# A gated delta recurrence on Trainium2: the level products of the inverses on 32x32 diagonal blocks instead of 64x64

## The chip, the core and the metric

The kernel runs on one core of a Trainium2 chip. The core has a matrix engine (TensorE, PE in the profile), which loads a stationary operand (PEld) and streams another through it into PSUM; VectorE (DVE), ScalarE (ACT) and GpSimd (POOL) for elementwise work; and SyncE (SP), which here only starts DMAs. The metric is the device time of the whole program in microseconds. All numbers are fp32.

## The reference

The program computes two blocks of two layers each on 1024 latent and 256 context tokens of width 1024. The first block's layers mix three branches; one is a bidirectional recurrence over the tokens, with 6 heads of 64 x 64 state, run forward and backward. Only this branch is touched:

```python
def _rwkv7_step(S, inp):
    r, w, k, v, kk, b = inp
    sa = jnp.einsum('bhvk,bhk->bhv', S, kk)
    S = S * w[:, :, None, :] - sa[..., None] * b[:, :, None, :] + v[..., None] * k[:, :, None, :]
    return S, jnp.einsum('bhvk,bhk->bhv', S, r)

def _rwkv_bidir(rin, S0_f, S0_b):
    r, decay, kd, v, kk, bd = rin
    S_f, y_f = lax.scan(_rwkv7_step, S0_f, (r, decay[:, :, 0], kd[:, :, 0], v, kk, bd[:, :, 0]))
    S_b, y_b = lax.scan(_rwkv7_step, S0_b, (r, decay[:, :, 1], kd[:, :, 1], v, kk, bd[:, :, 1]),
                        reverse=True)
    return S_f, S_b, y_f + y_b
```

## The kernel before

`rwkv_core` runs the recurrence once in each of the two layers of the first block. It cuts the 1280 tokens into chunks of 64 (`CH`), and takes them in 10 blocks of two chunks, with the forward and the backward direction (`d`) side by side. The heads go in three pairs (`g`, `NP = 3`); `h` is the head in its pair, `q = 2 d + h`, and `c` the chunk, which lies on 64 of the 128 partitions (`half[c]`).

Within a chunk the steps depend on each other through a strictly triangular 64x64 matrix A, and (1 + A) must be inverted. The kernel builds the inverse by doubling: level 0 is the identity with the 2x2 blocks' entries; level `lv` joins diagonal blocks of size 2^lv into ones of twice the size. `TU` holds for each q the current inverse T and its transpose U, `ML` the entries of A which belong to each level, cut out with masks by GpSimd (L2033). A level is

- `level_w` (L1778): W = (masked A)T, then ScalarE copies it from PSUM to `Ws` (L1942),
- `level_d` (L1793 and L1796): the two products of W with U, for T and for U, after which VectorE subtracts them from `TU` (L1971).

There are six levels (`NLEV = 6`), level 0 in GpSimd and 1 to 5 on TensorE; at level 5 only U is brought up to date. Around them a block has: `grams` (L1729), the products of the scaled keys that give A and three further 64x64 matrices, for the next block; `turned` (L1742, L1745), eight 128x128 transposes per head pair; `start_t` (L1753), T as the transpose of U at level 0; `bv` (L1764); `solve` (L1806), the inverse times X; `outputs` (L1826 to L1841), the products that make the block's transfer matrices; and `state` (L1857, L1865), which applies the block before to the carried state and its outputs.

Each engine's program is written out by hand, in the order in which the functions `block_of` call the steps; nothing reorders it. On TensorE the ten blocks are unrolled completely. A level is W of pair 0, W of pair 1, D of 0, W of 2, D of 1, D of 2; the state's first half follows level 1 and its second level 3, and the three gram groups of the next block follow levels 2 to 4. Semaphores are counted waits: `pw`/`aw` between W and ScalarE, `pd`/`dl` between D and VectorE, `pn`/`dh` and `py`/`dy` for the state. SyncE loads a block's operands (`rk_in`, six DMAs of 384 KB, and smaller ones) as soon as the outputs two blocks earlier are done.

## Time and profile before

| | |
|---|---|
| median of 3 runs | 4876.69 us (4873.02 to 4878.9) |
| profiled execution, its span | 4866.1 us |
| TensorE matmuls busy | 4241.5 us, 87% |
| TensorE weight loads busy | 3280.6 us, 67% |
| VectorE busy | 2749.5 us, 57% |
| ScalarE, GpSimd busy | 1537.1 us, 1475.8 us |
| instructions recorded | 103654 |

The profile is of one execution; its own time isn't recorded apart from the span, and the median of the runs lies 10.6 us above the span. The two recurrences run in the stretches from about 555 to 1030 us and from 2118 to 2592 us. "PE" counts matmuls from first column in to last out, so that several overlap in the array and a busy TensorE is not one at its peak: how closely starts follow each other tells more. A line such as `L1793 ... 64*64 64x64 x4` is a group of four records with a 64x64 stationary operand and 64 rows by 64 columns streamed. "issue" as a releaser means that the engine waited for nothing that the profile shows. Instructions reach the engines from memory through DMA queues of their own, queue 8 among them.

### The profile page before, as it was taken

The numbers are of one execution on the slowest core, as the hardware profiler recorded it, in microseconds if no ns is written. First come the engines' busy times: TensorE is split into PE (matmuls) and PEld (weight loads), VectorE is DVE, ScalarE is ACT, GpSimd is POOL, SyncE is SP. The second block draws the span as 40 slices with busy tenths as digits, with TensorE's granted clock in tenths as the row PEclk, the third lists the DMA queues.
The fourth block names the chain that finished last, engine by engine and source line by source line (L and its number), as shares of the span: only waits on it lengthen the run. The fifth ranks groups of instructions, "written<-read, shape, count | busy, mean of one in ns | idle before, by whom it ended". The sixth has DMA issues, their size and how long they took to land. (4 is left out here: it accounts for less than half of the span.)

```text
span 4866.1 us, 103654 instructions
## 1 busy us (share of the span) xinstructions
PE 4241.5 (87%) x43026; PEld 3280.6 (67%) x43026; DVE 2749.5 (57%) x4666; ACT 1537.1 (32%) x2721; POOL 1475.8 (30%) x1090
## 2 busy tenths in 40 slices
PE   6999889877998799989986998689788988978898
PEld 4887688854667587778884666578545677854566
DVE  3465444455666447544445665665575656557565
ACT  1332222223552123222222553210155421015542
POOL 2232233302013323233331111565232135523213
PEclk8999999988999899989998999789899999989999
DMA  6455532342135445642324133533403253340325
GB/s 194 146 186 189 145 78 59 81 159 83 42 83 178 148 153 198 197 122 71 78 59 148 45 92 112 172 99 106 149 7 81 67 183 124 104 142 17 81 53 181
DMA packets 517941, 561.41 MB, mean 115 GB/s; under 512 B 112732, under 2 KB 412284, under 8 KB 515380
## 3 DMA queue, kind: packets, MB, share of 16 engines
q1 hardware_dynamic: 389876, 475.93, 31.6%
q10 hardware_dynamic: 127616, 78.95, 5.6%
q8 instruction: 348, 5.70, 0.5%
q14 instruction: 101, 0.83, 0.1%
HBM read 366.75 MB, written 192.23 MB: 115 GB/s over the span
## 5 line engine op out<-in xcount | busy, mean ns | idle before, releaser
L1096 PE MATMUL pr_acc<-hH,pr_wh 128*128 128x512 f32 (+1 forms) x1288 | 482.4, 375 | 0.0
L1097 PE MATMUL pr_acc<-hL,pr_wh 128*128 128x512 f32 (+1 forms) x1288 | 466.0, 362 | 0.0
L1098 PE MATMUL pr_acc<-hH,pr_wl 128*128 128x512 f32 (+1 forms) x1288 | 465.6, 361 | 0.0
L2586 ACT ACTIVATE an_p<-an_p,an_stat 128x1280 f32<-128x1280 f32 (+5 forms) x372 | 339.7, 914 | 162.8 <-DVE an_stat L2664 157.2
L2033 POOL TENSOR_TENSOR rk_ml<-rk_lmask,rk_g 128x384 f32<-128x384 f32 x240 | 232.1, 999 | 464.1 <-DVE rk_g L1963 464.1
L2526 PE MATMUL an_t<-ident,an_p 128*128 128x128 f32 x2152 | 319.5, 283 | 40.3 <-ACT an_pT L2593 27.8
L2619 POOL TENSOR_TENSOR an_kl<-an_k,an_kh 128x1280 fp32r<-128x1280 f32 (+3 forms) x36 | 78.5, 2179 | 898.5 <-DVE an_qh L2644 898.5
L2526 PEld LDWEIGHTS an_t<-ident,an_p 128*128 128x128 f32 x2152 | 236.7, 142 | 163.9 <-issue 68.0
L2660 DVE CUSTOM_DVE_ANT_0 an_p<-an_s,an_mask 128x256 f32<-128x256 f32 (+8 forms) x308 | 274.9, 892 | 101.7 <-PE an_s L2509 68.4
L1971 DVE TENSOR_TENSOR rk_tu<-rk_tu,rk_ps 128x512 f32<-128x512 f32 x300 | 190.3, 634 | 237.0 <-PE rk_ps L1796 237.0
L1465 POOL TENSOR_TENSOR sp_sl<-sp_w,sp_sh 128x512 fp32r<-128x512 f32 x172 | 246.0, 1437 | 196.8 <-DVE sp_sh L1540 178.4
L2551 PE MATMUL an_oacc<-an_pT,an_v 128*64 128x512 f32 (+3 forms) x1224 | 298.1, 562 | 4.0 <-DVE an_pT L2671 1.9
L1374 PE MATMUL sp_acc<-sp_ch,sp_sh 128*128 128x512 f32 x728 | 285.5, 392 | 7.6 <-POOL sp_sl L1465 7.6
L1140 POOL TENSOR_TENSOR pr_wl<-pr_w,pr_wh 128x1024 fp32r<-128x1024 f32 x58 | 142.7, 2461 | 470.1 <-DVE pr_wh L1160 470.1
L1375 PE MATMUL sp_acc<-sp_cl,sp_sh 128*128 128x512 f32 x728 | 285.1, 392 | 0.0
L1376 PE MATMUL sp_acc<-sp_ch,sp_sl 128*128 128x512 f32 x728 | 284.9, 391 | 0.0
L1096 PEld LDWEIGHTS pr_acc<-hH,pr_wh 128*128 128x128 f32 x1288 | 245.4, 191 | 58.0 <-issue 20.5
L2593 ACT COPY an_pT<-an_t 128x512 f32<-128x512 f32 (+3 forms) x356 | 186.2, 540 | 297.2 <-PE an_t L2526 296.3
L1796 PE MATMUL rk_ps<-rk_tu,rk_ws 64*64 64x64 f32 x4800 | 276.7, 219 | 3.5 <-issue 3.3
L1097 PEld LDWEIGHTS pr_acc<-hL,pr_wh 128*128 128x128 f32 x1288 | 245.3, 190 | 38.0 <-issue 1.0
L1098 PEld LDWEIGHTS pr_acc<-hH,pr_wl 128*128 128x128 f32 x1288 | 244.6, 190 | 38.1
L2671 DVE COPY an_pT<-an_t 128x512 f32<-128x512 f32 (+3 forms) x256 | 155.7, 616 | 178.5 <-PE an_t L2526 176.0
(382 smaller groups left out, 10181.1 us busy)
## 6 DMA issues: line engine op xcount, KB each, us to landing
CHK<-ri_out SPq DMA_DIRECT2D x24, 1920.0 KB, 8.1
rk_in<-CHK SPq DMA_DIRECT2D x120, 384.0 KB, 5.9
pr_w<-in_w_in ACTq DMA_DIRECT2D x58, 512.0 KB, 4.1
UT<-pr_out SPq DMA_DIRECT2D x45, 640.0 KB, 4.6
sp_w<-in_w_in ACTq DMA_DIRECT2D x50, 512.0 KB, 5.2
U<-sp_c SPq DMA_DIRECT2D x100, 256.0 KB, 2.0
mod_w<-in_w_mod SPq DMA_DIRECT2D x16, 1024.0 KB, 8.0
mo_w<-in_w_out SPq DMA_DIRECT2D x16, 1024.0 KB, 9.6
```

The costliest lines, as they stand in the source:

```text
L1096: nc.tensor.matmul(out, wh[:, u, k, 0:m], hi, start=(k == 0), stop=False)
L1097: nc.tensor.matmul(out, wh[:, u, k, 0:m], lo, start=False, stop=False)
L1098: ins = nc.tensor.matmul(out, wl[:, u, k, 0:m], hi, start=False, stop=(k == KT - 1))
L1374: nc.tensor.matmul(to, sH[:, a, k, :], cH[:, i, k, :], start=(k == 0), stop=False)
L1375: nc.tensor.matmul(to, sH[:, a, k, :], cL[:, i, k, :], start=False, stop=False)
L1376: ins = nc.tensor.matmul(to, sL[:, a, k, :], cH[:, i, k, :], start=False, stop=(k == H - 1))
L1465: g.tensor_tensor(sL[:, slot(q, i)], weight(q, i), sH[:, slot(q, i)], ALU.subtract).then_inc(w_lo.sem, 1)
L1796: ins = nc.tensor.matmul(o[half[c], q, 1, :], Ws[half[c], g, q, :], TU[half[c], u, g, q, 1, :], start=True, stop=True)
L2526: ins = nc.tensor.transpose(bank[:, j * P:(j + 1) * P], Pm[:, n % NPM, j, col:col + P], ident[:])
L2551: ins = nc.tensor.matmul(O[half * HD:(half + 1) * HD, cs], V[:, c % 2, blocks[n][k], :], PT[:, buffer(n, k), cs], start=(p == 0), stop=(p ...
L2586: nc.scalar.activation(row, row, ACT.Exp, bias=stat[:, n % NPM, j, 1:2], scale=heads[groups[n][0]].scale, accum_out=total[:, n % 4, j:j + ...
L2660: V_.tensor_tensor_reduce(out=Pm[:, n % NPM, j, 0:width], in0=scores_at(m, width), in1=extra, scale=1.0, scalar=-3.0e38, op0=ALU.add, op1= ...
```

## The change

The levels 1 to 4 now work on 32x32 diagonal blocks (`QB = 32`), four on the partitions (`quarter`), each product being one of 32 rows and columns, so `ML`, `TU` and `Ws` have 32 columns. Twice as many products do each W and D. The last level, the join of two 32x32 halves into one 64x64, becomes a step of its own (`join`): W is formed from the unmasked far corner of A with half as many outputs, and `LU` receives, negated by VectorE, the 32 x 64 strip of the inverse that the joining changes. `solve` uses `LU` (64 rows) for one half of the outputs and `TU` (32 rows) for the other. `grams` computes A's columns in two 32-column parts, near and far, by 32x32 outputs, and the other three matrices as before. GpSimd makes the masks of both heads in one instruction, for five levels of 32 columns.

In addition the function `between` puts the state and gram products of a level behind its second W and ahead of its first D (before: behind its last D), and VectorE's state and mask steps now stand ahead of the level's subtractions. One table more, `eye`, is loaded.

```diff
 NLEV = 6
+QB = CH // 2
...
-        ML = core.sb(s, "rk_ml", [P, 2, NP, 2, 2, NLEV, CH])
-        TU = core.sb(s, "rk_tu", [P, 2, NP, 4, 2, CH])
-        Ws = core.sb(s, "rk_ws", [P, NP, 4, CH])
+        ML = core.sb(s, "rk_ml", [P, 2, NP, 2, 2, NLEV - 1, QB])
+        TU = core.sb(s, "rk_tu", [P, 2, NP, 4, 2, QB])
+        LU = core.sb(s, "rk_lu", [P, NP, 2, 2, QB])
+        Ws = core.sb(s, "rk_ws", [P, NP, 4, QB])
...
+
+        def join_at(g):
+
+            i = 6 if g == 1 else 4
+            return banks[:, i * 512:(i + 2) * 512].rearrange("p (d k) -> p d k", d=2)[:, :, 0:2 * QB].rearrange("p d (h k) -> p d h k", h=2)
...
-                        for j, arr in enumerate((A_BH, A_KH)):
+                        for far in range(2):
+                            for i in range(4):
+                                for h in range(2):
+                                    o = bank[h][quarter[i], d * 256 + far * QB:d * 256 + (far + 1) * QB]
+                                    nc.tensor.matmul(o, D[half[h], u, g, d, A_BH, quarter[i]], D[half[h], u, g, d, A_KT, quarter[i ^ far]],
+                                                     start=True, stop=True)
+                        for arr, a0, n, at0 in ((A_BH, A_RT, 1, CH), (A_KH, A_KT, 2, P)):
                             for c in range(2):
                                 for h in range(2):
-                                    rows, tok = half[h], half[c]
-                                    o = bank[h][half[c], d * 256 + j * P:d * 256 + (j + 1) * P]
-                                    ins = nc.tensor.matmul(o, D[rows, u, g, d, arr, tok], D[rows, u, g, d, A_KT:A_RT + 1, tok],
+                                    o = bank[h][half[c], d * 256 + at0:d * 256 + at0 + n * CH]
+                                    ins = nc.tensor.matmul(o, D[half[h], u, g, d, arr, half[c]], D[half[h], u, g, d, a0:a0 + n, half[c]],
                                                            start=True, stop=True)
                     ins.then_inc(pg.sem, 1)
...
                     for q in range(4):
-                        for c in range(2):
-                            ins = nc.tensor.matmul(wbank(u, g)[half[c], q * CH:(q + 1) * CH], TU[half[c], u, g, q, 1, :],
-                                                   pair[half[c], :], start=True, stop=True)
+                        for i in quarter:
+                            ins = nc.tensor.matmul(wbank(u, g)[i, q * QB:(q + 1) * QB], TU[i, u, g, q, 1, :], eye[i, 0, :],
+                                                   start=True, stop=True)
                     ins.then_inc(pw.sem, 1)
...
@@ -1774,9 +1789,15 @@
                     pe.wait_ge(aw.sem, aw.nth(NW * b + k - 1))
                     for q in range(4):
                         d, h = q // 2, q % 2
-                        for c in range(2):
-                            ins = nc.tensor.matmul(wbank(u, k)[half[c], q * CH:(q + 1) * CH], ML[half[c], u, g, d, h, lv, :],
-                                                   TU[half[c], u, g, q, 0, :], start=True, stop=True)
+                        if lv < NLEV - 1:
+                            for i in quarter:
+                                ins = nc.tensor.matmul(wbank(u, k)[i, q * QB:(q + 1) * QB], ML[i, u, g, d, h, lv, :],
+                                                       TU[i, u, g, q, 0, :], start=True, stop=True)
+                        else:
+                            for c in range(2):
+                                i, far = quarter[2 * c + d], quarter[2 * c + 1 - d]
+                                ins = nc.tensor.matmul(wbank(u, k)[far, h * QB:(h + 1) * QB], G[i, u, g, d, h, 0, QB:CH],
+                                                       TU[i, u, g, q, 0, :], start=True, stop=True)
                     ins.then_inc(pw.sem, 1)
...
                         pe.wait_ge(dl.sem, dl.nth(ND * b + n - 1))
-                    o = dbank(n).rearrange("p (q a k) -> p q a k", q=4, a=2)
+                    o = dbank(n)[:, 0:8 * QB].rearrange("p (q a k) -> p q a k", q=4, a=2)
                     for q in range(4):
-                        if lv < NLEV - 1:
+                        for i in quarter:
+                            nc.tensor.matmul(o[i, q, 0, :], TU[i, u, g, q, 1, :], Ws[i, g, q, :], start=True, stop=True)
+                        for i in quarter:
+                            ins = nc.tensor.matmul(o[i, q, 1, :], Ws[i, g, q, :], TU[i, u, g, q, 1, :], start=True, stop=True)
+                    ins.then_inc(pd.sem, 1)
+
+                def join(b, u, g):
+
+                    n = ND - NP + g
+                    pe.wait_ge(aw.sem, aw.nth(NW * b + NW - 2 * NP + g + 1))
+                    if g == 0:
+                        pe.wait_ge(dl.sem, dl.nth(ND * b + n))
+                    elif g == 1:
+                        pe.wait_ge(dh.sem, dh.nth(2 * b))
+                        pe.wait_ge(dy.sem, dy.nth(2 * b))
+                    else:
+                        pe.wait_ge(dl.sem, dl.nth(ND * b + n - 1))
+                    o = join_at(g)
+                    for h in range(2):
+                        for d in range(2):
                             for c in range(2):
-                                nc.tensor.matmul(o[half[c], q, 0, :], TU[half[c], u, g, q, 1, :], Ws[half[c], g, q, :],
-                                                 start=True, stop=True)
-                        for c in range(2):
-                            ins = nc.tensor.matmul(o[half[c], q, 1, :], Ws[half[c], g, q, :], TU[half[c], u, g, q, 1, :],
-                                                   start=True, stop=True)
+                                i, far = quarter[2 * c + d], quarter[2 * c + 1 - d]
+                                nc.tensor.matmul(o[i, d, h, :], Ws[far, g, h, :], TU[far, u, g, 2 * d + h, 1, :], start=True, stop=True)
+                                ins = nc.tensor.matmul(o[far, d, h, :], eye[far, 1, :], TU[far, u, g, 2 * d + h, 1, :],
+                                                       start=True, stop=True)
                     ins.then_inc(pd.sem, 1)
...
@@ -1802,17 +1841,20 @@
                     pe.wait_ge(dl.sem, dl.nth(ND * b + ND - NP + g + 1))
                     pe.wait_ge(aw.sem, aw.nth(NW * b + k - 1))
                     for q in range(4):
+                        d, h = q // 2, q % 2
                         for c in range(2):
-                            ins = nc.tensor.matmul(wbank(u, k)[half[c], q * P:(q + 1) * P], TU[half[c], u, g, q, 1, :],
-                                                   X[half[c], g, q, :], start=True, stop=True)
+                            near, far = quarter[2 * c + d], quarter[2 * c + 1 - d]
+                            nc.tensor.matmul(wbank(u, k)[far, q * P:(q + 1) * P], LU[half[c], g, d, h, :], X[half[c], g, q, :],
+                                             start=True, stop=True)
+                            ins = nc.tensor.matmul(wbank(u, k)[near, q * P:(q + 1) * P], TU[near, u, g, q, 1, :], X[near, g, q, :],
+                                                   start=True, stop=True)
                     ins.then_inc(pw.sem, 1)
...
-                    for lv in range(1, NLEV):
-                        level_w(b, u, lv, 0)
-                        level_w(b, u, lv, 1)
-                        level_d(b, u, lv, 0)
-                        level_w(b, u, lv, 2)
-                        level_d(b, u, lv, 1)
-                        level_d(b, u, lv, 2)
-                        first = isinstance(b, int) and b == 0
+                    first = isinstance(b, int) and b == 0
+
+                    def between(lv):
                         if lv == 1 and not first:
                             pe.wait_ge(atx.sem, atx.nth(2 * (NP * b + NP)))
                             pe.wait_ge(dbk.sem, dbk.nth(NP * b + NP))
@@ -1893,6 +1930,20 @@
                             state(b - 1, 1 - u, 1)
                         if more and lv >= 2 and lv - 2 < NP:
                             grams(b + 1, 1 - u, lv - 2)
+                    for lv in range(1, NLEV):
+                        level_w(b, u, lv, 0)
+                        level_w(b, u, lv, 1)
+                        between(lv)
+                        if lv < NLEV - 1:
+                            level_d(b, u, lv, 0)
+                            level_w(b, u, lv, 2)
+                            level_d(b, u, lv, 1)
+                            level_d(b, u, lv, 2)
+                        else:
+                            join(b, u, 0)
+                            level_w(b, u, lv, 2)
+                            join(b, u, 1)
+                            join(b, u, 2)
                     solve(b, u, 0)
...
-                    both = slice(0, 2) if lv < NLEV - 1 else slice(1, 2)
-                    o = TU[:, u, g, :, both, :]
-                    nc.vector.tensor_tensor(o, o, dbank(n).rearrange("p (q a k) -> p q a k", q=4, a=2)[:, :, both, :],
-                                            ALU.subtract).then_inc(dl.sem, 1)
+                    if lv < NLEV - 1:
+                        o = TU[:, u, g, :, :, :].rearrange("p q a k -> p (q a k)")
+                        nc.vector.tensor_tensor(o, o, dbank(n)[:, 0:8 * QB], ALU.subtract).then_inc(dl.sem, 1)
+                    else:
+                        nc.vector.tensor_scalar(LU[:, g], join_at(g), -1.0, None, ALU.mult).then_inc(dl.sem, 1)
...
@@ -2004,14 +2057,14 @@
                     for lv in range(1, NLEV):
                         if lv == 1:
                             dve.wait_ge(aw.sem, aw.nth(NW * b + NP))
-                        for g in range(NP):
-                            level(b, u, lv, g)
                         if lv == 1 and not first:
                             state(b - 1, 1 - u, 0)
                         if lv == 3 and not first:
                             state(b - 1, 1 - u, 1)
                         if more and lv >= 2 and lv - 2 < NP:
                             masked(b + 1, 1 - u, lv - 2)
+                        for g in range(NP):
+                            level(b, u, lv, g)
...
                         for d in range(2):
-                            for h in range(2):
-                                ins = nc.gpsimd.tensor_tensor(ML[:, u, g, d, h, :, :], lm[:, d, :, :],
-                                                              G[:, u, g, d, h, 0:1, :].to_broadcast([P, NLEV, CH]), ALU.mult)
+                            ins = nc.gpsimd.tensor_tensor(ML[:, u, g, d], lm[:, d, :, :].unsqueeze(1).to_broadcast([P, 2, NLEV - 1, QB]),
+                                                          G[:, u, g, d, :, 0:1, 0:QB].to_broadcast([P, 2, NLEV - 1, QB]), ALU.mult)
```

TensorE, level 1 of the second block and the state products, before (L1778 is W, L1793 and L1796 are D, L1857 and L1865 the state):

```order
L1778 MATMUL rk_ps<-rk_tu,rk_ml 64x64 x8
L1793 MATMUL rk_ps<-rk_ws,rk_tu 64x64 x2
L1796 MATMUL rk_ps<-rk_tu,rk_ws 64x64 x2
L1793 MATMUL rk_ps<-rk_ws,rk_tu 64x64 x2
...
L1793 MATMUL rk_ps<-rk_ws,rk_tu 64x64 x2
L1796 MATMUL rk_ps<-rk_tu,rk_ws 64x64 x2
L1857 MATMUL rk_ps<-rk_h,rk_mn 64x64 x12
L1865 MATMUL rk_ps<-rk_qy,rk_h 64x64 x12
L1778 MATMUL rk_ps<-rk_tu,rk_ml 64x64 x16
L1793 MATMUL rk_ps<-rk_ws,rk_tu 64x64 x2
```

The same place after (L1794 is W, L1813 and L1815 are D, L1899 and L1907 the state):

```order
L1794 MATMUL rk_ps<-rk_tu,rk_ml 32x32 x32
L1899 MATMUL rk_ps<-rk_h,rk_mn 64x64 x12
L1907 MATMUL rk_ps<-rk_qy,rk_h 64x64 x12
L1813 MATMUL rk_ps<-rk_ws,rk_tu 32x32 x4
L1815 MATMUL rk_ps<-rk_tu,rk_ws 32x32 x4
L1813 MATMUL rk_ps<-rk_ws,rk_tu 32x32 x4
...
L1794 MATMUL rk_ps<-rk_tu,rk_ml 32x32 x16
L1813 MATMUL rk_ps<-rk_ws,rk_tu 32x32 x4
```

The state products moved from behind the last D to between the second W and the first D; a W of one pair went from 8 products to 16, and D from groups of two to groups of four.

VectorE at the same place, before (L2002 copies transposes, L1971 is the level, L1991 and L1996 the state, L1963 the masking of the grams):

```order
L2002 COPY rk_bk<-rk_ps 128x512 x3
L1971 TENSOR_TENSOR rk_tu<-rk_tu,rk_ps 128x512 x3
L1991 TENSOR_TENSOR rk_h<-rk_ps,rk_mn 128x384
L1996 TENSOR_TENSOR rk_qy<-rk_ps,rk_qy 128x3x2x64
L1971 TENSOR_TENSOR rk_tu<-rk_tu,rk_ps 128x512 x3
L1963 TENSOR_TENSOR rk_g<-rk_ps,rk_mask 128x2x256 x2
```

And after (L2055, L2023, L2044, L2049 and L2015 in the same roles):

```order
L2055 COPY rk_bk<-rk_ps 128x512 x3
L2044 TENSOR_TENSOR rk_h<-rk_ps,rk_mn 128x384
L2049 TENSOR_TENSOR rk_qy<-rk_ps,rk_qy 128x3x2x64
L2023 TENSOR_TENSOR rk_tu<-rk_tu,rk_ps 128x256 x3
L2015 TENSOR_TENSOR rk_g<-rk_ps,rk_mask 128x2x256 x2
L2023 TENSOR_TENSOR rk_tu<-rk_tu,rk_ps 128x256 x3
```

The state's two additions and the next gram mask now come ahead of the three level subtractions, which have 256 elements a partition instead of 512.

TensorE at the first solve, before (L1806 is the solve, L1796 the last D):

```order
L1796 MATMUL rk_ps<-rk_tu,rk_ws 64x64 x16
L1806 MATMUL rk_ps<-rk_x,rk_tu 64x128 x16
L1826 MATMUL rk_ps<-rk_g,rk_tx 64x64 x4
L1829 MATMUL rk_ps<-rk_g,rk_tx 64x64 x4
L1832 MATMUL rk_ps<-rk_g,rk_v 64x64 x4
```

And after (L1834 and L1835 are the join, L1847 the far part of the solve with 64 rows, L1849 the near part with 32):

```order
L1834 MATMUL rk_ps<-rk_tu,rk_ws 32x32
L1835 MATMUL rk_ps<-rk_tu,rk_eye 32x32
L1847 MATMUL rk_ps<-rk_x,rk_lu 32x128
L1849 MATMUL rk_ps<-rk_x,rk_tu 32x128
L1847 MATMUL rk_ps<-rk_x,rk_lu 32x128
L1849 MATMUL rk_ps<-rk_x,rk_tu 32x128
```

One product over 64 rows became two, and these alternate in the number of their rows.

## Rows read from the trace of the kernel before

**Rows 1.** The profile's page: span, TensorE's busy time, the instruction queue's packets

```profile
span 4866.1 us, 103654 instructions
PE 4241.5 (87%) x43026; PEld 3280.6 (67%) x43026; DVE 2749.5 (57%) x4666; ACT 1537.1 (32%) x2721; POOL 1475.8 (30%) x1090
q8 instruction: 348, 5.70, 0.5%
```

**Rows 2.** Busy time in each window: us, PE, PEld, DVE, ACT, POOL, PEclk, DMA, GB/s

```profile
555.00:1030.00 475.00, 420.75 (x13106) 396.43 (x13107) 218.62 (x395) 115.55 (x300) 156.85 (x190) 0.96 0.28 71
2118.00:2592.00 474.00, 424.23 (x13214) 400.19 (x13216) 221.50 (x402) 115.56 (x300) 156.90 (x190) 0.96 0.28 71
```

**Rows 3.** Timeline, TensorE at block starts: start, us, line, tiles, count, [idle before]

```profile
575.66 0.69 PE L1742 MATMUL rk_ps<-ident,rk_in 128*128 128x128 f32 x2
...
990.20 0.66 PE L1742 MATMUL rk_ps<-ident,rk_in 128*128 128x128 f32 x2 [1.59 <-DVE rk_mn L1983]
...
2136.86 0.69 PE L1742 MATMUL rk_ps<-ident,rk_in 128*128 128x128 f32 x2
...
2548.02 0.41 PE L1742 MATMUL rk_ps<-ident,rk_in 128*128 128x128 f32 x2 [1.55 <-DVE rk_mn L1983]
```

**Rows 4.** Timeline of the weight loads in a level, two tiles in turn

```profile
778.40 0.55 PEld L1778 LDWEIGHTS rk_ps<-rk_tu,rk_ml 64*64 64x64 f32 x16
778.87 0.20 PEld L1793 LDWEIGHTS rk_ps<-rk_ws,rk_tu 64*64 64x64 f32 x4
778.98 0.20 PEld L1796 LDWEIGHTS rk_ps<-rk_tu,rk_ws 64*64 64x64 f32 x4
```

**Rows 5.** Timeline of the weight loads in the outputs, four tiles in turn

```profile
752.02 0.21 PEld L1832 LDWEIGHTS rk_ps<-rk_g,rk_v 64*64 64x64 f32 x8
752.14 0.21 PEld L1835 LDWEIGHTS rk_ps<-rk_bk,rk_tx 64*64 64x64 f32 x8
```

**Rows 6.** Timeline of the weight loads, inside the outputs of a later block

```profile
804.11 0.14 PEld L1829 LDWEIGHTS rk_ps<-rk_g,rk_tx 64*64 64x64 f32 x2
806.19 0.14 PEld L1829 LDWEIGHTS rk_ps<-rk_g,rk_tx 64*64 64x64 f32 x2 [1.95 <-issue]
```

**Rows 7.** Busy time in windows from one such resumption to the next

```profile
802.28:806.18 3.90, 2.10 (x128) 1.95 (x127) 1.41 (x4) 0.00 (x0) 0.00 (x0) 1.00 0.02 4
707.73:711.34 3.61, 2.10 (x128) 1.95 (x127) 1.42 (x4) 0.00 (x0) 0.00 (x0) 1.00 0.02 5
753.67:757.61 3.94, 2.68 (x128) 2.59 (x127) 1.42 (x4) 0.60 (x1) 0.00 (x0) 1.00 0.02 4
893.28:897.19 3.91, 2.09 (x128) 1.95 (x127) 1.48 (x5) 0.00 (x0) 0.00 (x0) 1.00 0.01 4
```

**Rows 8.** DMA queue 8 (packets, MB, share) in 555:1030, then in 776:803

```profile
q8 instruction: 104, 1.70, 1.5%
...
q8 instruction: 7, 0.11, 1.7%
```

**Rows 9.** Busy time in a stretch of levels and outputs, and behind a block's loads

```profile
776.50:800.00 23.50, 23.49 (x780) 22.75 (x779) 12.99 (x21) 5.66 (x14) 13.60 (x15) 1.00 0.08 22
761.00:768.00 7.00, 7.00 (x152) 6.37 (x152) 2.08 (x3) 4.38 (x13) 1.91 (x4) 1.00 0.93 217
```

**Rows 10.** Timeline, TensorE: transposes, the products behind them, and a later gap

```profile
763.50 0.60 PE L1745 MATMUL rk_ps<-ident,rk_in 128*128 128x128 f32 x4
764.03 0.68 PE L1753 MATMUL rk_ps<-rk_pair,rk_tu 64*64 64x64 f32 x16
...
769.81 0.33 PE L1793 MATMUL rk_ps<-rk_ws,rk_tu 64*64 64x64 f32 x4 [1.59 <-issue]
```

**Rows 11.** Groups by line with shapes apart: a product of 32 rows elsewhere

```profile
L583 PE MATMUL side_acc<-ri_lrt,ri_lowrank 32*128 32x320 f32 x192 | 64.3, 454 | 0.0
```

**Rows 12.** Timeline, ScalarE: the copies of two W results in a level

```profile
777.05 0.84 ACT L1942 COPY rk_ws<-rk_ps 128x256 f32<-128x256 f32 x2 [5.21 <-PE rk_ps L1778]
```

**Rows 13.** Busy time in a window at the lower clock

```profile
808.90:812.30 3.40, 3.40 (x40) 2.95 (x39) 0.69 (x1) 1.16 (x4) 1.54 (x4) 0.50 0.72 198
```

29 lines of the change are left out of this document (18 added, 11 removed).

## The prediction

> **What bounds the kernel now.** I read the page first: the span is 4866.1 us in the profiled execution, the runs' median is 4876.7, so some 10.6 us lie around the span; the change doesn't touch them, and I add differences to the median. TensorE is busy for 87% of the span, but the change touches only the two stretches in which the recurrence runs, one for each layer. The busy times of these windows come next [rows 2]: 475 and 474 us, with VectorE busy 46%, GpSimd 33% and ScalarE 24% of them. So TensorE, or what feeds it, sets the time there. The timeline gives the period of a block (two chunks forward, two backward, all heads): the first transposes of blocks 0 and 9 start at 575.66 and 990.20 in layer 0, and at 2136.86 and 2548.02 in layer 1 [rows 3]. That is 46.1 and 45.7 us a block, 45.9 in the mean, with 10 blocks in a layer and 20 in all.
>
> Then I looked at how fast weight loads, each with its matmul, follow each other. In a level, where the tiles alternate between two 64x64 quarters of the array, 16 pairs take 778.87 - 778.40 = 0.47 us, 29 ns a pair [rows 4]. In the outputs, where four tiles take turns, 8 pairs take 0.12 us, 15 ns a pair [rows 5]. Both are the same 58 to 60 ns for each tile. An fp32 product is two pairs, so four instructions; a transpose is one pair.
>
> By that the outputs should fly, and they don't: in the middle of a row of products that wait for nothing, weight loads stop at 804.11 and go on at 806.19, with "issue" as the releaser [rows 6]. Four windows from the end of one such gap, or the restart at it, to the next all hold 128 pairs, which is 256 instructions, and last 3.90, 3.61, 3.94 and 3.91 us, of which TensorE is busy for 2.1 to 2.7 [rows 7]. The whole program moved 348 packets, 5.70 MB, on the instruction queue [rows 1]: 16 KB a packet, or 256 instructions of 64 bytes. The number fits TensorE alone: 43026 matmuls and as many loads, with its waits, make some 89,000 instructions, 348 times 256. So TensorE gets its program in portions of 256, and in none of these windows did a portion come faster than 3.6 us after the last. The queue shows it for a longer stretch too: 7 packets between 776 and 803, one in 3.86 us, and 104 in the recurrence of a layer [rows 8]. In levels the array itself needs 128 x 29 ns = 3.7 us for a portion: array and supply are just level with each other, and 780 pairs take 23.5 us, 30 ns each [rows 9].
>
> **The change, part by part.** Counted from the code, a block has 672 products before: 48 gram, 24 transposes, 24 start of T, 24 for bv, 120 W, 216 D, 24 solve, 144 outputs, 48 state. After it there are 1128: grams 144, start 48, W 216 (16 a head pair on four levels, 8 on the last), D and join 432, solve 48, the rest as before. That is 456 more, all fp32, and a 32-row product still has two pairs: L583, of 32 rows, stands 96 times in the program and 192 times in the trace [rows 11].
>
> Array time alone: 360 products (start, W, D) at two tiles cost 58 ns each, 20.9 us a block. Their 696 successors rotate over four 32x32 tiles. No row shows a 32-wide stream. I bound it above by what four 64-wide tiles take, 30 ns a product [rows 5], so 20.9 us again, and below by half of that, 10.4, for half the width. The grams were 48 products of 128 columns over four tiles, 60 ns each at twice the width, 2.9 us; they become 96 small ones, 24 of 64 and 24 of 128 columns, at most 5.0 us and at least 3.6. So the array gains up to 10 us a block, or loses 2.
>
> Supply: 456 x 4 = 1824 instructions are 7.1 portions. Today's count is 104 packets in 10 blocks, 10.4; it becomes 17.5. At 3.85 us each (the mean of the four windows is 3.84, the long stretch gives 3.86) today's supply takes 40.0 of the 45.9 us, so 5.9 us a block are not covered by it. I can name them: 1.6 us at each block's start, where the first transposes wait for VectorE's last outputs [rows 3]; the transposes, 152 pairs in 7.0 us where supply needs 4.6; and the portion asked for while the block's loads fill the DMA engines (share 0.93), which comes late, with a gap of 1.6 us [rows 9, 10]. After: 17.5 x 3.85 = 67.4 us. Of the 5.9 the transposes' excess mostly goes, because start of T now brings 48 more pairs to the same stretch; the start and the late portion stay. I take 4.0, between 2 and 5.9.
>
> Order on TensorE: state and gram products of a level move in front of its first D. They fill the time in which ScalarE copies W, 0.84 us for two [rows 12], which is worth something only if TensorE would stand there with instructions at hand. With supply as the limit it is worth nothing: a level has 144 products, 2.2 portions, 8.7 us, against 0.84 us for its copies. The state products wait for VectorE and for the last copies of the transposes; behind them on TensorE the level's D is now queued, and for D VectorE's subtractions. The state's operands were ready a level earlier than it was run before, so I price this wait at nothing; one longer than the supply's slack would cost that much once a block. VectorE's level subtraction falls from 512 to 256 elements, its state and mask steps come ahead of it, and ScalarE's copies halve; all of this and GpSimd's fewer masks lie beside 72 us of TensorE. They are worth nothing, at most the 2 us that separates my 4.0 from the lower bound; without a supply limit rival A lives on them. SP has one small load more, before the first block.
>
> Solve: far and near products alternate between 64 and 32 rows, 16 changes a head pair, 48 a block. The nearest row is the change from 128-wide transposes to 64-wide products: the last of four transposes starts near 763.83 (0.60 us for four, about 0.27 for one) and the next product at 764.03 [rows 10], 0.2 us where transposes follow at 0.11. So a change costs 0 to 0.1 us, 0 to 4.8 us a block, partly within the supply's 2.9 us for these 48 products. I take 0.7. The Trainium skill's TensorEngine Tiling (Array Packing), Key Properties, says that changing the tiling mode drains the engine, which speaks against this mix of sizes; by a full drain at each change the sum would be near the upper end, and this trace can't show more than the 0.1 us.
>
> Sum: 67.4 + 4.0 + 0.7 = 72.1 us a block against 45.9, so 26.2 more; times 20 that is +524 us, and 4876.7 + 524 = 5401. Its own range: 17.5 x 3.6 + 2 = 65.0 gives +382; 17.5 x 3.94 + 5.9 + 3 = 77.9 gives +640.
>
> **The rivals.** A, not slower: the gaps at 256 instructions are an effect of something else in the outputs, and the supply keeps up. Then the place that decides is the levels' and grams' array time, -10 to +2 us a block, with the new order filling the wait behind W. For the gaps' cause being elsewhere speaks that levels show few of them; against it, that the portion of 128 pairs comes back in each window to the pair, and that levels run at just the 30 ns a pair where supply would hold them. I take -5 us a block: 4777, between 4677 and 4917. It decides as soon as a pair costs less than (45.9 - 4.7) us / 2232 pairs = 18 ns over the whole block (4.7 being the uncovered time of the main case), where supply gives 30.
> The Trainium skill's Runtime: NRT & Kernel Launch, Instruction fetch mechanics, takes this side: the sequencer streams its 16 KB blocks by itself and crossing one is mostly hidden, since dispatch is slower than the fill. The trace agrees on the 16 KB and disagrees on hidden, by rows 6 and 7; by that rule rival A's 4777 would be the time.
>
> B, slower still: with TensorE's array idle half of each portion, the granted clock falls to 1.2 GHz. In the recurrence it is 0.96 [rows 2], and 0.50, the lower of the two levels, from 808.9 to 812.3, right behind the gap at a block's start, in which the engine had stood still [rows 13]. At half clock the outputs take 144 x 60 ns = 8.6 us, still within supply's 8.7; state and bv, 72 products at 0.12 us, are 8.6 us where supply needs 4.3; transposes at 0.22 us, 24 of them, are 5.3 us and no longer hidden by 1 to 2. Together some 6 us a block, +120: 5521.
>
> C, the portion comes faster when it alone is asked for: the shortest window is 3.61, and with the array half idle and 2 us uncovered a tenth less, 3.3, is thinkable: 59.8 us a block, +278: 5155. No row shows 3.3.
>
> **How the numbers follow.** Main case 0.65, A 0.11, B 0.15, C 0.08, and 0.01 for no change. The time is the main case's, 5401. The range takes in the main case's own 5259 to 5517 and leans a little to C: 5220 to 5520. About 0.2% is what a measurement of this kernel can tell from no change; that is 10 us. A lies mostly below it: faster 0.09, same 0.02, slower 0.89.
>
> **What would show it.** Right: about 175 packets of queue 8 in each recurrence stretch, one in 3.8 to 3.9 us; the 32-wide products in bursts well under 29 ns a pair, broken by "issue" gaps of 1 to 3 us every 128 pairs, now in the levels too; a block period near 72 us; everything outside the two stretches within a few us. Solve wrong: its 96 pairs take much over 3 us apart from a gap. Wrong altogether: a period under 50 us, or packets at 2.5 us apart; then the supply was never the limit. B is seen in the granted clock of the two stretches, near 0.5 to 0.7 instead of 0.96.

## The result and the profile after

The changed kernel takes 5780.74 us (median of 4 runs, 5775.97 to 5792.86), the kernel before, in the same comparison, 4874.85 us: a ratio of 1.186 [1.184, 1.188], 906 us more. The direction and the cause named first were right; the size was not: 5401 was forecast, in a range that ended at 5520. The execution that was profiled took 5792.86 us, the longest of the four.

The page of the kernel after, its span, TensorE's busy time, the granted clock in 40 slices, the instruction queue, and two of its groups; what answers to it is in [rows 1]:

```profile
span 5791.1 us, 139996 instructions
PE 4811.8 (83%) x61266; PEld 3436.3 (59%) x61266; DVE 2673.5 (46%) x4666; ACT 1495.0 (26%) x2721; POOL 1328.3 (23%) x970
PEclk8998666666699989985656667998898899998899
q8 instruction: 491, 8.04, 0.6%
L1813 PE MATMUL rk_ps<-rk_ws,rk_tu 32*32 32x32 f32 x7680 | 225.0, 223 | 106.4 <-issue 105.9
L1847 PE MATMUL rk_ps<-rk_x,rk_lu 64*32 64x128 f32 x960 | 291.1, 403 | 0.0
L1849 PE MATMUL rk_ps<-rk_x,rk_tu 32*32 32x128 f32 x960 | 290.3, 401 | 0.1
```

The program has 491 packets on queue 8 instead of 348: 143 more, 7.1 a block, as counted ahead. There are 18240 more matmuls, which is 456 products of two passes in 20 blocks. L1813, a product of a level's D, stood 106 us behind "issue". The two solve lines are the surprise: 1920 passes of some 400 ns each, 581 us busy in sum.

TensorE's timeline at the first and the last block of each layer (start, us, line, tiles, count, [idle before]), which answers to [rows 3]:

```profile
580.57 0.69 PE L1757 MATMUL rk_ps<-ident,rk_in 128*128 128x128 f32 x2
...
1411.86 0.41 PE L1757 MATMUL rk_ps<-ident,rk_in 128*128 128x128 f32 x2 [1.59 <-DVE rk_mn L2036]
...
2595.53 0.69 PE L1757 MATMUL rk_ps<-ident,rk_in 128*128 128x128 f32 x2
...
3422.37 0.41 PE L1757 MATMUL rk_ps<-ident,rk_in 128*128 128x128 f32 x2 [1.59 <-DVE rk_mn L2036]
```

The period of a block is (1411.86 - 580.57) / 9 = 92.4 us and (3422.37 - 2595.53) / 9 = 91.9, 92.1 in the mean, where it was 45.9. 20 times the 46.2 us is 924, and the span grew by 925: all of the loss lies in the two recurrences.

The weight loads of the kernel after, in a level, which answer to [rows 4 and 6]:

```profile
959.52 0.20 PEld L1813 LDWEIGHTS rk_ps<-rk_ws,rk_tu 32*32 32x32 f32 x8 [3.54 <-issue]
959.60 0.23 PEld L1815 LDWEIGHTS rk_ps<-rk_tu,rk_ws 32*32 32x32 f32 x8
959.70 0.23 PEld L1813 LDWEIGHTS rk_ps<-rk_ws,rk_tu 32*32 32x32 f32 x8
959.81 0.23 PEld L1815 LDWEIGHTS rk_ps<-rk_tu,rk_ws 32*32 32x32 f32 x8
...
960.77 0.54 PEld L1794 LDWEIGHTS rk_ps<-rk_tu,rk_ml 32*32 32x32 f32 x31
963.52 0.59 PEld L1794 LDWEIGHTS rk_ps<-rk_tu,rk_ml 32*32 32x32 f32 x30 [2.22 <-issue]
```

Eight loads take 0.10 to 0.11 us, 13 ns a pair, where two 64-wide tiles in turn took 29 and four took 15. The latter two were at the granted clock 1.00, this one is at 0.50, as the windows below show. The burst ends after less than 2 us, and the engine waits for nothing that the profile shows until 963.52. Windows of the kernel after (us, PE, PEld, DVE, ACT, POOL, PEclk, DMA, GB/s), first three portions from resumption to resumption, answering to [rows 7], then most of a layer, answering to [rows 2]:

```profile
959.52:963.52 4.00, 1.92 (x127) 1.79 (x127) 0.84 (x2) 0.00 (x0) 0.00 (x0) 0.50 0.02 4
963.52:967.46 3.94, 3.25 (x127) 2.33 (x127) 0.00 (x0) 0.53 (x2) 0.00 (x0) 0.50 0.02 4
971.33:975.46 4.13, 1.93 (x128) 1.80 (x128) 0.84 (x2) 0.00 (x0) 0.43 (x1) 0.50 0.02 4
590.00:1500.00 910.00, 686.96 (x21774) 459.01 (x21773) 175.89 (x391) 90.20 (x286) 74.68 (x117) 0.63 0.12 32
2600.00:3510.00 910.00, 690.98 (x21918) 465.78 (x21914) 177.03 (x393) 92.62 (x294) 75.80 (x120) 0.62 0.12 32
```

Again 128 pairs, one record short in two of them, in 3.9 to 4.1 us. In two of the three the array is busy for half of that (1.9 us), in the other for 3.25 us. The granted clock fell from 0.96 to 0.63: for much of the stretch it is 0.50, the lower level of 1.2 GHz. That was rival B's sign.

The solve is in another state altogether. Its timeline and a window of the kernel after:

```profile
1003.73 0.63 PE L1847 MATMUL rk_ps<-rk_x,rk_lu 64*32 64x128 f32 x2
1004.29 0.63 PE L1849 MATMUL rk_ps<-rk_x,rk_tu 32*32 32x128 f32 x2
1004.85 0.63 PE L1847 MATMUL rk_ps<-rk_x,rk_lu 64*32 64x128 f32 x2
1005.41 0.63 PE L1849 MATMUL rk_ps<-rk_x,rk_tu 32*32 32x128 f32 x2
```

```profile
1003.70:1021.70 18.00, 18.00 (x77) 5.69 (x68) 0.39 (x2) 0.60 (x1) 0.00 (x0) 0.50 0.01 2
```

One product (two passes) starts every 0.56 us, with no gap that any row calls idle. 48 of them would be 26.9 us a block; the starts of all 20 blocks give 25.7 us in the mean, because part of the third pair's solve runs at a higher clock in half of the blocks. 3.6 us, supply and changes together, had been set down. A busy TensorE (18.00 of 18.00 us) hides this: the busy time counts latencies, and only the distance of the starts tells that one product runs at a time, where the solve of the kernel before had two tiles in turn and 0.11 us a product.

### The profile page after: what moved, and what is told of

Read it like the earlier page. It is cut to its first block and busy times, and to the rows that moved or that the text cites. A ratio compares the mean times of both kernels' runs of the same rounds, so it can differ in the third digit from the quotient of the medians.

```text
span 5791.1 us, 139996 instructions
## 1 busy us (share of the span) xinstructions
PE 4811.8 (83%) x61266; PEld 3436.3 (59%) x61266; DVE 2673.5 (46%) x4666; ACT 1495.0 (26%) x2721; POOL 1328.3 (23%) x970
## 5 line engine op out<-in xcount | busy, mean ns | idle before, releaser
L2034 DVE TENSOR_TENSOR rk_qy<-rk_ps,rk_in 128x256 f32<-128x256 f32 x120 | 50.3, 419 | 600.9 <-PE rk_ps L1883 600.9
L1813 PE MATMUL rk_ps<-rk_ws,rk_tu 32*32 32x32 f32 x7680 | 225.0, 223 | 106.4 <-issue 105.9
L1994 ACT COPY rk_ws<-rk_ps 128x128 f32<-128x128 f32 x300 | 76.3, 254 | 879.2 <-PE rk_ps L1794 766.7
L1815 PE MATMUL rk_ps<-rk_tu,rk_ws 32*32 32x32 f32 x7680 | 224.3, 223 | 89.7 <-issue 89.6
L2085 POOL TENSOR_TENSOR rk_ml<-rk_lmask,rk_g 128x320 f32<-128x320 f32 x120 | 100.6, 859 | 840.5 <-DVE rk_g L2015 840.5
L1847 PE MATMUL rk_ps<-rk_x,rk_lu 64*32 64x128 f32 x960 | 291.1, 403 | 0.0
L1849 PE MATMUL rk_ps<-rk_x,rk_tu 32*32 32x128 f32 x960 | 290.3, 401 | 0.1
L1813 PEld LDWEIGHTS rk_ps<-rk_ws,rk_tu 32*32 32x32 f32 x7680 | 194.2, 135 | 125.9 <-issue 123.6
```

Source lines behind the costliest of these rows:

```text
L1813: nc.tensor.matmul(o[i, q, 0, :], TU[i, u, g, q, 1, :], Ws[i, g, q, :], start=True, stop=True)
L1847: nc.tensor.matmul(wbank(u, k)[far, q * P:(q + 1) * P], LU[half[c], g, d, h, :], X[half[c], g, q, :], start=True, stop=True)
L1849: ins = nc.tensor.matmul(wbank(u, k)[near, q * P:(q + 1) * P], TU[near, u, g, q, 1, :], X[near, g, q, :], start=True, stop=True)
```

## Experiments

Medians of the runs, ratio to the kernel before as it ran in the same comparison, with its 95% interval, and the period of a block and the packets of queue 8 a block. Both come from the trace, from the first transposes of block 0 to those of block 9, in the mean of the two layers:

| kernel | us | ratio | period, us | packets |
|---|---|---|---|---|
| before | 4874.85 | 1 | 45.9 | 10.5 |
| after | 5780.74 | 1.186 [1.184, 1.188] | 92.1 | 17.6 |
| before, new order | 4877.84 | 1.001 [1.000, 1.002] | 46.2 | 10.5 |
| after, solve grouped | 5371.68 | 1.102 [1.100, 1.105] | 70.8 | 17.6 |
| grouped, W products doubled | 5590.52 | 1.148 [1.145, 1.151] | 82.3 | 20.6 |
| grouped, old order | 5374.77 | 1.102 [1.099, 1.104] | 71.6 | 17.6 |
| grouped, T turned by VectorE | 5166.03 | 1.059 [1.056, 1.061] | 60.3 | 13.8 |
| before, small products alternating | 4962.74 | 1.019 [1.016, 1.021] | 50.7 | 10.6 |
| before, small products grouped | 4891.32 | 1.005 [1.004, 1.007] | 46.5 | 10.7 |
| before, loads spread | 4885.95 | 1.004 [1.002, 1.005] | 46.7 | 10.5 |
| before, T turned by VectorE | 4777.53 | 0.980 [0.978, 0.982] | 41.0 | 8.6 |
| T by VectorE, new order | 4794.43 | 0.984 [0.982, 0.986] | 41.7 | 8.6 |
| T by VectorE, new order, two banks | 4743.20 | 0.973 [0.971, 0.974] | 39.4 | 8.6 |
| T by VectorE, old order, two banks | 4722.00 | 0.968 [0.966, 0.969] | 38.7 | 8.6 |

"Grouped" is the changed kernel with its solve grouped; the last four rows are variants of the kernel before.

### The order alone

The kernel before, with state and gram products ahead of a level's first D on TensorE, and VectorE's steps ahead of its subtractions:

```diff
+                    def between(lv):
                         if lv == 1 and not first:
...
                     for lv in range(1, NLEV):
                         level_w(b, u, lv, 0)
                         level_w(b, u, lv, 1)
+                        between(lv)
                         level_d(b, u, lv, 0)
```

> The 64x64 products of the kernel before, with only the new order: state and gram products between a level's second W and its first D on TensorE, and VectorE's state and mask steps ahead of the level's subtractions. Theory 'supply and alternation' (TensorE gets its instructions in portions of 256, none sooner than 3.6 us after the last, and the solve's alternating 64- and 32-row products each wait for the one before): the order is worth 0 to -1.5 us of 45.9 us a block, so 4845 to 4880. Rival 'order' (the state's waits, now ahead of D, hold up the level chain, and this is where the 906 us come from in part): slower, 5 us a block or more, 4975 or above.

4877.84 us, within the bound of what can be told from no change. The order is worth nothing where supply sets the time.

### The solve grouped

The changed kernel, where a head pair's solve does its eight far products first (64 rows, `LU`) and then its eight near ones (32 rows, `TU`): one change of size inside a pair instead of 15, with the same products.

```diff
-                    for q in range(4):
-                        d, h = q // 2, q % 2
-                        for c in range(2):
...
+                    for near_part in range(2):
+                        for q in range(4):
+                            d, h = q // 2, q % 2
+                            for c in range(2):
```

> The changed kernel, with the solve's 8 far products (64 rows) of a head pair first and its 8 near products (32 rows) behind them, the same products otherwise. Supply and alternation: the solve's 48 products fall from 0.56 us each, 26.9 us a block, to what supply gives them, 2.9 us, with 6 changes of row size at 0.5 us or less; -21 to -24 us a block, 5300 to 5370. Rival 'clock' (the products are slow because the granted clock is 0.5 there, and 128 columns at 1.2 GHz take it): grouping changes little, 5700 or above. Rival 'order': no change from it, 5780.

5371.68 us, 2 us above the 5300 to 5370 expected: 409 less than the changed kernel, 21.3 us a block in the traces. The timeline of the kernel with the solve grouped, first the third pair of a block, whose clock is 1.00, then the first two pairs of the next block, and a window over these two and one over most of a layer:

```profile
641.52 0.65 PE L1852 MATMUL rk_ps<-rk_x,rk_lu 64*32 64x128 f32 x16
642.10 0.65 PE L1849 MATMUL rk_ps<-rk_x,rk_tu 32*32 32x128 f32 x16
...
705.46 1.09 PE L1852 MATMUL rk_ps<-rk_x,rk_lu 64*32 64x128 f32 x16
706.48 1.09 PE L1849 MATMUL rk_ps<-rk_x,rk_tu 32*32 32x128 f32 x16
707.50 1.09 PE L1852 MATMUL rk_ps<-rk_x,rk_lu 64*32 64x128 f32 x16
708.52 1.08 PE L1849 MATMUL rk_ps<-rk_x,rk_tu 32*32 32x128 f32 x16
```

```profile
705.46:709.54 4.08, 4.08 (x71) 2.49 (x65) 0.36 (x2) 0.60 (x1) 0.00 (x0) 0.51 0.02 4
590.00:1215.00 625.00, 421.20 (x19762) 352.72 (x19760) 158.53 (x351) 81.20 (x257) 72.91 (x113) 0.69 0.18 45
```

At the granted clock 1.00, 16 passes, eight products, need 642.10 - 641.52 = 0.58 us, 73 ns a product. At 0.50, the clock at which the alternating ones took 560 ns each, they need 706.48 - 705.46 = 1.02 us, 127 ns a product. So at the same low clock the grouping alone makes a product over four times as fast, and rival 'clock' falls as the main cause. Over the starts of all 20 blocks the solve takes 5.4 us a block instead of 25.7: 20.3 us of array time went, and 21.3 showed. With that place mended the kernel stands near where the rest of the forecast had put it: 70.8 us a block against 72.1, 5372 against 5401. The clock is still 0.69 over most of a layer, which suggests that a low clock by itself costs little outside the solve.

### Small products among the solve's of the kernel before

To price a change in the other kernel, near full clock: eight more products of 32 rows, whose results nothing reads, in the third pair's solve; once one ahead of each of the eight 64-row products (15 changes inside the pair), once all eight in front (one change).

```diff
+                    def small(q):
+                        nc.tensor.matmul(bank[4][0:32, q * P:(q + 1) * P], TU[0:32, u, g, q, 1, 0:32], X[0:32, g, q, :], start=True, stop=True)
                     for q in range(4):
                         for c in range(2):
+                            if g == 2 and True:
+                                small(q)
                             ins = nc.tensor.matmul(wbank(u, k)[half[c], q * P:(q + 1) * P], TU[half[c], u, g, q, 1, :],
```

> The kernel before, with eight small products (32 rows by 32 columns, 128 streamed, result unused) added to the third head pair's solve of each block, one ahead of each 64-row product, so that row sizes alternate: 16 changes a block. Alternation: each product waits until the one before it has left the array, 0.3 to 0.56 us each instead of 0.11, so 16 products cost 5 to 9 us where 0.9 stood: +4 to +8 us a block, +80 to +160 us against before, and +70 to +150 against the same products grouped. Rival 'clock' (a change of row size costs little at the full clock, and the changed kernel's 0.56 us come from the half clock): within 20 us of the grouped kernel.

```diff
+                    if g == 2:
+                        for q in range(8):
+                            nc.tensor.matmul(bank[4][0:32, q % 4 * P:(q % 4 + 1) * P], TU[0:32, u, g, q % 4, 1, 0:32], X[0:32, g, q % 4, :],
+                                             start=True, stop=True)
                     for q in range(4):
```

> The same eight small products a block, all ahead of the third head pair's 64-row products: 2 changes of row size. Supply: 32 instructions are 0.13 portions, 0.5 us a block; with two changes at 0.3 to 0.5 us +0.5 to +1.5 us a block, +10 to +30 us against before under both theories.

4962.74 and 4891.32 us, 71 us apart with the same products: 3.6 us a block, 0.25 us for each of the 14 changes (by the traces' periods, 4.2 us and 0.30). First the timeline and the window of the kernel with small products alternating, then those of the one with them grouped:

```profile
614.93 0.40 PE L1805 MATMUL rk_ps<-rk_x,rk_tu 32*32 32x128 f32 x2
615.26 0.43 PE L1810 MATMUL rk_ps<-rk_x,rk_tu 64*64 64x128 f32 x2
615.62 0.40 PE L1805 MATMUL rk_ps<-rk_x,rk_tu 32*32 32x128 f32 x2
```

```profile
614.93:620.30 5.37, 5.37 (x47) 2.58 (x45) 1.42 (x4) 0.00 (x0) 0.00 (x0) 1.00 0.00 0
```

```profile
613.47 1.93 PE L1806 MATMUL rk_ps<-rk_x,rk_tu 32*32 32x128 f32 x16
615.33 0.97 PE L1810 MATMUL rk_ps<-rk_x,rk_tu 64*64 64x128 f32 x13
```

```profile
613.47:616.15 2.68, 2.68 (x40) 2.42 (x36) 1.42 (x4) 0.00 (x0) 0.00 (x0) 1.00 0.00 0
```

At the granted clock 1.00 an alternating product starts 0.33 to 0.36 us after the last. The single records behind these groups have the second pass 0.13 or 0.16 us after the first, and the next product's first pass 0.20 after that; grouped, passes on one tile follow at 0.11. So the change itself adds about 0.09 us, and the rest is that the product's two passes have the array alone, one after the other. In the changed kernel, at 0.50, the two distances are 0.21 and 0.35: about 0.13 for the change, and 0.43 for two passes of 128 columns. That is the failed step taken apart. Every second 64-row product lies on rows and columns that the small tile doesn't touch, and its distances are the same; so it isn't that two products want the same part of the array. Of the 3.6 us a block, 5.37 - 2.68 = 2.7 lie in this stretch. Part of the rest is the clock: over the 20 blocks the alternating stretch runs at granted clocks from 0.70 to 1.00 and takes 6.0 us in the mean, up to 7.0, while the grouped one has 1.00 and 2.7 us in every block. That is 3.3 us of the 3.6.

### The price of a portion

The kernel with the solve grouped, every W product of levels 1 to 4 issued twice to the same place: 192 products, 768 instructions, 3 portions more a block.

```diff
-                            for i in quarter:
+                            for i in quarter + quarter:
```

> The kernel with the grouped solve, in which each W product of levels 1 to 4 is issued twice into the same place (the result is the same): 192 more products a block, 768 instructions, 3.0 portions. Supply: 3.0 x 3.85 = 11.6 us a block more than with the grouped solve alone, +231 us. Array: at 13.3 ns a pair (0.106 us for 8 pairs in the changed kernel's trace) 192 x 2 x 13.3 = 5.1 us, which lies in time in which TensorE now stands idle if it is a wait on ScalarE or VectorE that ends it: 0 to +100 us.

5590.52 us, 219 more where supply alone gives 231. Its page:

```profile
q8 instruction: 551, 9.03, 0.7%
```

60 packets more, 3.0 a block, and by the periods 11.5 us: 3.84 us a portion. By the medians of the runs it is 219 / 60 = 3.65 us. By the 13 ns of a pair the array would have needed 192 x 2 x 13 ns = 5.0 us, and less where it stands idle anyway. The supply is the bound of the levels, within 5% of the price read from the trace before.

### The late portion

The kernel before, with SyncE holding back the loads of pairs 1 and 2 until the block before has reached its first and fourth level result, to take the DMA burst from beside the transposes:

```diff
                     for g in range(NP):
+                        if g and later:
+                            sp.wait_ge(dl.sem, dl.nth(ND * (b - 1) + (1 if g == 1 else 4)))
                         for d in range(2):
```

> The kernel before, with the block loads of head pairs 1 and 2 held back by SyncE until level 1 and level 2 of the running block have begun, instead of all six going out at the block's start; nothing else changes. Supply, with the portion asked for beside the loads coming late (the gap of 1.6 us at 769.81): that gap goes, 1 to 2 us a block, -20 to -40 us. Rival (that gap is not from the loads, or another wait lies under it): within 10 us of before.

4885.95 us, 0.35% [0.21, 0.48] slower instead of 20 to 40 us faster. TensorE's timeline of the kernel with loads spread, through its levels:

```profile
770.48 0.33 PE L1795 MATMUL rk_ps<-rk_ws,rk_tu 64*64 64x64 f32 x4 [1.04 <-ACT rk_ws L1944]
...
779.27 0.27 PE L1795 MATMUL rk_ps<-rk_ws,rk_tu 64*64 64x64 f32 x1 [0.81 <-issue]
...
784.98 0.27 PE L1795 MATMUL rk_ps<-rk_ws,rk_tu 64*64 64x64 f32 x3 [1.67 <-issue]
```

Of the packets of queue 8 behind these rows three follow each other at 771.62, 776.81 and 782.22: 5.2 and 5.4 us apart instead of 3.9, beside the shifted loads. The first of these intervals has the DMA engines busy for 0.57 of it, the second for 0.47. The other intervals say the same: in the first layer of the kernel before, those with the DMA engines busy for under 0.1 have a median of 3.9 us, and the 19 with over 0.4 one of 5.4 us, though many of these lie at block starts, where TensorE has other waits too. That loads delay a portion stands; that moving them pays fell. TensorE's idle time behind "issue" went from 4.0 to 4.4 us a block, and the block became 0.9 us longer. Why the loads cost more in their new place isn't shown.

### Fewer instructions

If the supply is the bound, the way forward is the opposite of the change. Up to level 4 the inverse is diagonal in 32x32 blocks, and VectorE's transpose turns each 32x32 block in its place, so it can make T from U. That drops `start_t` and the T half of D: 672 products become 552, 10.5 portions 8.6.

```diff
                     for q in range(4):
-                        if lv < NLEV - 1:
-                            for c in range(2):
-                                nc.tensor.matmul(o[half[c], q, 0, :], TU[half[c], u, g, q, 1, :], Ws[half[c], g, q, :],
-                                                 start=True, stop=True)
...
+                def turn_t(b, u, g):
+                    nc.vector.transpose(TU[:, u, g, :, 0, :], TU[:, u, g, :, 1, :]).then_inc(dt.sem, 1)
```

> The kernel before with fewer TensorE instructions: T is taken from U by VectorE's transpose of 32x32 blocks (up to level 4 both have entries only inside these), so that start of T and the T half of D at levels 1 to 4 go: 120 of 672 products a block, 480 instructions, 1.9 portions, and 15 transposes of 256 elements come on VectorE, which was busy 46%. Supply: -1.9 x 3.85 = -7.2 us a block, -144 us; by the array's 58 ns a product -7.0, the same. If the longer chain between levels (a subtraction and a transpose, some 0.8 us) is uncovered on four levels, 3 us of it is lost: -80. Rival 'levels are bound by their chain of waits, not by TensorE's instructions': no gain or slower.

4777.53 us, 97 less than before: 4.9 us a block for 1.9 portions, which by supply alone are 7.2. Part of what is missing stands at the block's start. TensorE's timeline of this kernel:

```profile
737.13 0.41 PE L1743 MATMUL rk_ps<-ident,rk_in 128*128 128x128 f32 x2 [1.56 <-issue]
...
739.07 0.66 PE L1743 MATMUL rk_ps<-ident,rk_in 128*128 128x128 f32 x2 [0.87 <-DVE rk_bk L1982]
```

Without `start_t` between them the second pair's transposes wait 0.87 us for the first's to be copied from the same two PSUM banks; together such waits are 1.0 us a block. Three kernels follow from that. The new order on top, as in the first experiment:

```diff
                         level_w(b, u, lv, 1)
+                        between(lv)
                         level_d(b, u, lv, 0)
```

> The kernel with VectorE's transposes for T, and the new order (state and gram products between a level's second W and first D, VectorE's state and mask steps ahead of its subtractions). Supply: with TensorE's instructions fewer, 8.5 portions in 40.6 us a block, the chain of a level is no longer covered, and filling the wait behind W is worth 0 to 2 us a block: 0 to -40 us against the same kernel in the old order (4777). Rival: the order is worth nothing here either, within 10 us of it.

4794.43 us: 17 slower, where 0 to 40 less was expected. Once supply leaves more of the time to others, the order isn't free any more, and its sign is against it. It brings a wait that the old order doesn't have: a D (L1781) waits for VectorE's subtraction of an earlier D, which frees its PSUM bank. Of TensorE's waits over 578 to 955, 9 blocks (us in total, times, longest):

```profile
PE rk_ps L1781 <- DVE rk_tu L1948: 11.1, 26, 0.4
```

That is 1.2 us a block; by the periods the new order costs 0.7. Then the second pair's transposes in two other banks:

```diff
+        def tbank(g, part):
+            return bank[(2 if g == 1 else 6) + part]
...
-                    pe.wait_ge(atx.sem, atx.nth(2 * (NP * b + g)))
-                    pe.wait_ge(dbk.sem, dbk.nth(NP * b + g))
+                    if g == 2:
+                        pe.wait_ge(atx.sem, atx.nth(2 * (NP * b + 1)))
+                        pe.wait_ge(dbk.sem, dbk.nth(NP * b + 1))
```

> As that one, and the second head pair's transposes go to two PSUM banks of their own, so that they don't wait for the copies of the first (the gap of 1.1 us at 779.80 in the trace of the kernel with VectorE's transposes). Theory: about 1 us a block less, -20 us against the kernel with transposes and the new order. Rival (the portion that comes late behind the block's loads sets the end of this stretch anyway): no change.

4743.20 us, 51 less where 20 was expected, 2.3 us a block by the periods. The wait for `rk_bk`, 1.0 us a block, is gone, and so is the one for `rk_mn` at the block's start, 0.4; what the rest is remains open. And the same banks in the old order:

```diff
                         level_w(b, u, lv, 1)
-                        between(lv)
                         level_d(b, u, lv, 0)
```

> VectorE's transposes and the two extra banks, with the order of the kernel before. From the runs so far the new order cost 17 us with VectorE's transposes (4794 against 4777) and the banks saved 51: 4715 to 4735, ratio about 0.970. If the order's cost came from the same stretch as the banks' saving, the two don't add and it is within 5 us of 4743.

4722.00 us, 3.2% [3.1, 3.4] faster than before, and the best of all kernels here. The period is 45.9 - 38.7 = 7.2 us less, about what supply gives for 1.9 portions, and the wait of D for VectorE has gone with the new order. The block's start in its timeline has the wait for "issue" left (the wait for `rk_bk` is gone):

```profile
730.49 0.42 PE L1747 MATMUL rk_ps<-ident,rk_in 128*128 128x128 f32 x2 [1.56 <-issue]
```

### The grouped kernel without the order, and with fewer instructions

The order taken back, on TensorE and likewise on VectorE:

```diff
                         level_w(b, u, lv, 1)
-                        between(lv)
                         if lv < NLEV - 1:
...
                             join(b, u, 2)
+                        between(lv)
```

> The changed kernel with the grouped solve, and the old order: state and gram products behind a level's last D, VectorE's steps likewise. Supply bound: the order is worth nothing while TensorE waits for its portions, within 15 us of the grouped solve's 5372. Rival 'order' (moving them costs or gives something in the changed kernel): over 20 us away.

The changed kernel with the solve grouped and the old order takes 5374.77 us, 3 more than with the new one, where the intervals overlap. So the order explains nothing of the change in either kernel.

And T turned by VectorE in the grouped kernel:

```diff
                     for q in range(4):
                         for i in quarter:
-                            nc.tensor.matmul(o[i, q, 0, :], TU[i, u, g, q, 1, :], Ws[i, g, q, :], start=True, stop=True)
-                        for i in quarter:
                             ins = nc.tensor.matmul(o[i, q, 1, :], Ws[i, g, q, :], TU[i, u, g, q, 1, :], start=True, stop=True)
```

> The changed kernel with the grouped solve, and T taken from U by VectorE's 32x32 transposes, so that start of T and the T half of D go: 240 of 1128 products a block, 960 instructions, 3.75 portions. Supply: -3.75 x 3.85 = -14.4 us a block, -289 us against 5372: 5083, or up to 40 us more where the longer chain shows. Array: at 26 ns a product -6.2 us a block where the array is what is waited for, -125 us: 5247.

This kernel, in the new order, has 1128 - 240 = 888 products. 5166.03 us: 206 less, 10.6 us a block for 3.7 portions, 2.9 each. It lies between the two forecasts. The packets alone would give 14.2 us. Its waits (engine, line, releaser, us in total, times, longest) over 590 to 1100, 8.5 blocks:

```profile
PE rk_ps L1783 <- issue: 34.7, 21, 2.8
PE rk_ps L1802 <- issue: 33.2, 26, 2.5
PE rk_ps L1739 <- issue: 18.1, 11, 2.2
PE rk_ps L1758 <- issue: 9.4, 6, 1.6
PE rk_ps L1758 <- DVE rk_bk L2041: 8.3, 13, 0.9
```

"issue" still leads, so supply is still the main bound; about 1.0 us a block went to the same wait for the banks, 0.1 in the kernel it came from. The other 2.6 are not settled by a run.

## Why the prediction was wrong, step by step

**The count of portions: right.** 17.5 a block were worked out, 17.6 were found, and 348 + 143 = 491 in the whole program.

**The price of a portion: right.** 3.85 us was taken from four windows of the kernel before. Three portions added cost 3.84 us each by the periods (3.65 by the runs), in a stretch of 32-wide products that the kernel before didn't have. 1.9 portions taken away, with the banks, gave 7.2 us, 3.8 each. Rival A (supply keeps up, 4777) is dead.

The Trainium skill's Runtime: NRT & Kernel Launch, Instruction fetch mechanics, says that crossing a block of 16 KB is mostly hidden. The trace disagrees for this kernel: TensorE stands idle behind "issue" for 106 us at L1813 alone.

**What supply doesn't cover: nearly right.** 4.0 us was taken; the grouped kernel has 70.8 - 17.6 x 3.85 = 3.0. This is a remainder and not measured by itself, so errors of the other terms can hide in it.

**The array's own time for 32-wide tiles: inside the bounds.** 13 ns a pair is 27 ns a product, at the granted clock 0.50; the bounds were 15 and 30. At 1.00 it is faster. The weight loads of the grouped kernel, in a W:

```profile
1013.76 0.64 PEld L1794 LDWEIGHTS rk_ps<-rk_tu,rk_ml 32*32 32x32 f32 x64
```

That is 10 ns a pair, 20 ns a product. This time never decided.

**The order: right at nothing**, shown in both kernels.

**The clock: half of rival B.** It fell to 0.63, as B said and the main case did not. But B's price, 6 us a block for state, bv and transposes, is not seen: the grouped kernel has nearly the same clock, 0.69, and comes in below the main case. The place found where the low clock costs is the solve, where the array itself is the bound and which B didn't name: a product there would take 0.35 us at the full clock, 16.6 us a block for 48, and the 48 took 25.7 us in the mean. So some 9 of the 46.2 us a block that the change lost are the clock's, by this estimate; no run shows the changed kernel at the full clock.

**The solve: the step that failed.** "So a change costs 0 to 0.1 us, 0 to 4.8 us a block ... I take 0.7." The 0.1 us was not the error: the change itself adds 0.09 us at full clock and about 0.13 at half. The error is that I added a price per change to a stream whose products overlap. Those 48 products had 2.9 us as their supply, on the silent assumption that tiles still work side by side; with the changes 3.6 us was set down, and the solve took 25.7. That is the sign which the prediction had named as "Solve wrong". Between two changes there is one product, on one tile, with nothing beside it; so its two passes stand in full, 0.43 us at the low clock. The row I bounded by [rows 10] could not show it: it has one change between two long runs of one size, so it holds the 0.1 and none of the lost overlap. The right calculation was there to be made from rows of the page: 48 products alone, two passes of 128 columns each, in series. At 0.11 us a pass, the distance of transposes of 128 columns in [rows 10], and 0.1 a change, that is 0.32 us a product and 15.4 us a block, and twice the passes, 0.54 us and 26 us, at the clock of [rows 13]. It would have put the forecast at about 5640 with the one and 5850 with the other, with the measured 5781 between them.

The Trainium skill's TensorEngine Tiling (Array Packing), Key Properties, says that changing the tiling mode drains the engine. The trace nearly agrees: an alternating product starts 0.35 us after the last pass before it, and that pass is recorded for 0.42 us, so it has all but left; the ends of matmuls are modelled. I weighed it and put it "near the upper end", but worked out that end as 3 us more, which isn't a drain at 48 places. The rule spoke against just this mix of sizes, and deserved to be a rival with its own sum.

The whole account: 72.1 us a block forecast, 0.4 more for the portions (17.6 instead of 17.5), 1.0 less uncovered, without the 0.7 for changes, is the grouped kernel's 70.8; plus 21.3 for the alternating solve, 92.1. The 1.0 is the remainder from above, so the first sum closes by its making; the 21.3 is measured.

## What to carry to other kernels

With small fp32 products count instructions first: a portion of 256 costs TensorE 3.85 us here, so halving a product's size while doubling their number loses, and an operation that VectorE can take over wins. Group products by tile size instead of alternating them, since each alternation leaves a product alone on the array (0.35 us instead of 0.07 at the full clock, 0.56 instead of 0.13 at the low one). Where a cost is a loss of overlap, price the work in series, not a fee for each change; and a row can bound it only if it has the same pattern.
